# Two weight panels behind each norm multiplied with h times the scales, before the norm's factor is known

## The reference, cut to what matters

```
u = rmsnorm(h, gain) * (1 + scale) + shift      # factor = rsqrt(mean(h*h) + eps), one for each token
# feed-forward
h = h + 0.5 * (1 + gate) * ((silu(u @ wg) * (u @ wu)) @ wd)      # wg, wu: 1024 x 2816, wd: 2816 x 1024
# mixers
h = h + (1 + gate) * (mixers(u @ w_in) @ w_out)                  # w_in: 1024 x 5128
```

```
u @ w = factor * ((h * gain * (1 + scale)) @ w) + shift @ w
```

## Time and profile before

| | |
|---|---|
| median of 3 runs | 2034.93 us (2032.88 to 2040.63) |
| the profiled execution | 2039.97 us, of which the span of the profile is 2038.7 |
| mean granted clock of PE | 0.97 of full speed |
| busy: PE, DVE, ACT, POOL | 94%, 64%, 46%, 2% |
| instructions of PE | 15008 |
| DMA | 389.70 MB in 270996 packets, 57% of the engines' time in the main queue |

### The profile page before, as it was taken

The page is one execution under the profiler, slowest core; times in us unless marked ns, Lnnn a source line. Parts: engine busy times, 40 slices in busy tenths (PEclk is TensorE's granted clock), DMA queues, the critical chain, the costliest instruction groups (busy, mean ns, idle before and its releaser), DMA issues.

```text
span 2038.7 us, 33982 instructions
## 1 busy us (share of the span) xinstructions
PE 1909.3 (94%) x15008; PEld 1829.1 (90%) x15008; DVE 1311.0 (64%) x1850; ACT 942.6 (46%) x1266; POOL 43.7 (2%) x48
## 2 busy tenths in 40 slices
PE   7998988899898986999999899999999999899998
PEld 7987888898798885999899789999999999789998
DVE  4666677665776675666676856666666675755444
ACT  5564454446545443433445334334433446334333
POOL 0000100000000000000000000000000000000000
PEclk9998999999999998999989999999999999999999
DMA  9554456575363664677566345776677566334551
GB/s 291 171 190 149 160 192 223 162 256 176 129 218 127 213 216 158 210 248 249 183 214 220 134 136 186 248 248 227 211 250 248 181 212 202 104 124 145 187 186 63
DMA packets 270996, 389.70 MB, mean 191 GB/s; under 512 B 8448, under 2 KB 244224, under 8 KB 260480
## 3 DMA queue, kind: packets, MB, share of 16 engines
q1 hardware_dynamic: 270848, 387.52, 57.0%
HBM read 386.45 MB, written 1.05 MB: 190 GB/s over the span
## 4 chain that ended last, share of the span: by engine, by line
PE 69%; DVE 18%; ACT 10%; issue 1%; DMA 1%; POOL 1%; SPq 0%; DVEq 0%; ACTq 0%
PE bank L695 22%; PE bank L696 21%; PE bank L697 21%; DVE weights_split L844 6%; ACT weights_split L838 4%; PE bank L759 2%; ACT map L1279 1%; DVE xbc L2144 1%; DVE map_stat L1467 1%; ACT map L1285 1%; DVE weights L824 1%; PE bank L894 1%; DVE map L1461 1%; DVE work L792 0%; DVE a_qk_then_merged L1419 0%
## 5 line engine op out<-in xcount | busy, mean ns | idle before, releaser
L844 DVE TENSOR_TENSOR weights_split<-weights,weights_split 128x2048 fp32r<-128x2048 f32 (+2 forms) x306 | 655.2, 2141 | 434.1 <-ACT weights_split L838 433.6
L695 PE MATMUL bank<-u,weights_split 128*128 128x256 f32 x2048 | 589.7, 288 | 18.4 <-DVE u L2162 10.1
L838 ACT CAST weights_split<-weights 128x2048 fp32r<-128x2048 f32 (+2 forms) x306 | 543.1, 1776 | 136.4 <-PE bank L697 105.6
L696 PE MATMUL bank<-u,weights_split 128*128 128x256 f32 x2048 | 580.6, 283 | 0.0
L697 PE MATMUL bank<-u,weights_split 128*128 128x256 f32 x2048 | 579.5, 283 | 0.0
L695 PEld LDWEIGHTS bank<-u,weights_split 128*128 128x128 f32 x2048 | 392.0, 191 | 24.8 <-DVE u L2162 12.3
L696 PEld LDWEIGHTS bank<-u,weights_split 128*128 128x128 f32 x2048 | 394.0, 192 | 0.5 <-issue 0.5
L697 PEld LDWEIGHTS bank<-u,weights_split 128*128 128x128 f32 x2048 | 392.4, 192 | 0.0
L695 PE MATMUL bank<-y,weights_split 128*128 128x256 f32 (+1 forms) x1168 | 334.1, 286 | 4.2 <-ACT b_k L864 4.2
L696 PE MATMUL bank<-y,weights_split 128*128 128x256 f32 (+1 forms) x1168 | 330.8, 283 | 0.0
L697 PE MATMUL bank<-y,weights_split 128*128 128x256 f32 (+1 forms) x1168 | 330.0, 283 | 0.0
(11 more groups left out here) (285 smaller groups left out, 1898.5 us busy)
## 6 DMA issues: line engine op xcount, KB each, us to landing
weights<-in_ada SPq DMA_DIRECT2D x80, 1024.0 KB, 4.9
weights<-in_w_in SPq DMA_DIRECT2D x76, 1024.0 KB, 7.9
weights<-in_ffn_wg SPq DMA_DIRECT2D x44, 1024.0 KB, 5.4
weights<-in_ffn_wu SPq DMA_DIRECT2D x44, 1024.0 KB, 7.5
weights<-in_ffn_wd SPq DMA_DIRECT2D x44, 1024.0 KB, 7.2
weights<-in_w_merge SPq DMA_DIRECT2D x24, 1024.0 KB, 7.5
weights<-in_w_out SPq DMA_DIRECT2D x20, 1024.0 KB, 5.2
weights<-in_w_ple_gate SPq DMA_DIRECT2D x8, 1024.0 KB, 6.9
```

Source lines behind the costliest of these rows:

```text
L695: pe.matmul(out, left[0], right[0], start=start, stop=False, **more)
L696: pe.matmul(out, left[0], right[1], start=False, stop=False, **more)
L838: act.do.copy(split[:, 0, 0:n], raw[:, 0:n]).then_inc(*self.act_wrote.inc(("weights", key)))
L844: dve.do.tensor_tensor(split[:, 1, 0:n], raw[:, 0:n], split[:, 0, 0:n].bitcast(F32), ALU.subtract).then_inc(*self.dve_wrote.inc(("weights" ...
```

## The change

Two things are changed.

**The loads.** All weights of the plan are written into one array beforehand, panel after panel, as they stand in the buffer: a partition's part of a panel is one run of memory (8 KB for a full panel) where it was eight runs of 1 KB, or of 512 B for the panels of 128 columns.

**The norms of the six sub-layers** (not the last norm). The list has a new sequence, `boundary`:

- pending modulations are finished first (`pause_mods`)
- `raw`: for each chunk DVE adds to h, ACT rounds h times the scale into u (L2050) and squares h (L2056), DVE writes the low part (L2302). POOL adds the eight squares up (L2426). Two further columns of u hold the shifts, so a product gets the shift's share in column 256 (`u` has rows of 258 now)
- `deferred`: PE multiplies two panels at once, chunk by chunk, with this raw u, into four banks, 12 matmuls a chunk. Behind the fourth chunk it sums the squares over channels (one chunk now), behind the sixth it spreads the factor
- `modulated`: as before, but in place, u over the raw u chunk by chunk; the factor is copied out of its bank first (ACT, L2064)
- `deferred_out`: DVE copies the shift's share (L2340) and multiplies the banks by the factor (L2341); then silu and product (L2091, L2351) or copies and four convolutions with silu (L2080, L2274, L2277, L2034)
- only then `use` of the second panel, which puts the preparation of the fourth into the list

The panels are wg, wu number 0 of the feed-forwards and both of m_x for the mixers. The constants of the second model are loaded later and are waited for only by the mixers. Lines of the changed kernel: matmuls L717 to L719, a panel's cast L866 and low part L872, diagonal L820, modulations L852, adding to h L2285, u's chunks L2314, L2070, L2321.

The core of the diff:

```diff
+DEFERRED = {"ffn1": (("wg1", 0), ("wu1", 0)), "mix": (("m_x", 0), ("m_x", 1)), "ffn2": (("wg2", 0), ("wu2", 0))}
+
+SUMS_BEHIND, FACTORS_BEHIND = 3, 5
...
+    def boundary(self, before, name, l, at):
+        first, second = DEFERRED[name]
+        self.pause_mods()
         self.mods_until(72 * l + at + 2 * DC)
         self.add("coefficients", name, l, at)
-        self.run(self.norm(name, l))
+        self.add("raw", before, name, l, at)
+        self.use((*first[:1], l, *first[1:]))
+        for i in range(DC):
+            self.add("deferred", name, l, i)
+            if i == SUMS_BEHIND:
+                self.add("norm", (name, l), 0)
+            if i == FACTORS_BEHIND:
+                self.add("norm", (name, l), 1)
         self.add("modulated", name, l, at)
+        self.add("deferred_out", name, l)
+        self.use((*second[:1], l, *second[1:]))
+        self.mods_pause = False
...
-            kc = rows // P
-            sp.do.dma_start(slot[:, 0:kc * cols].rearrange("p (k n) -> p k n", k=kc),
-                            source.rearrange("(k p) n -> p k n", p=P)).then_inc(*loaded.inc((what, at)))
+            sp.do.dma_start(slot[:, 0:rows // P * cols], source).then_inc(*loaded.inc((what, at)))
...
+        if name in DEFERRED:
+            ring = self.products if name == "ffn2" else self.turned
+            return b["square_sum"], 1, 1, D, 1e-6, ring, [(self.pool_wrote, ("square_sum", tag))]
...
+        b["u_shift"] = sb("u", [P, DC, 2, T + 2], F32R)
+        b["u"] = b["u_shift"][:, :, :, 0:T]
+        b["square_sum"] = sb("square_sum", [P, 1, T])
+        b["factors"] = sb("factors", [P, T])
+        b["shift_product"] = sb("shift_product", [P, 4])
...
+    def deferred_rings(self, name):
+        if name == "ffn2":
+            return [self.scores, self.scores, self.turned, self.values]
+        return [self.products, self.products, self.spare_bank, self.values]
...
+            tag = {("wg1", 1): ("ffn1", l), ("wg2", 1): ("ffn2", l), ("m_bc", 0): ("mix", l)}.get((name, u))
+            if tag:
+                self.tensor_rows(key, b, t["u"], x_marks=[("u", tag, c) for c in range(DC)],
+                                 order=self.chunk_order(tag[0]))
...
+        pe.wait_ge(self.dve_wrote, ("raw", name, l, c))
+        for j, ring in enumerate(rings):
+            key, at = keys[j // 2], slice(j % 2 * P, (j % 2 + 1) * P)
+            hi, lo, _, _ = self.panel(key)
+            if i == 0:
+                pe.wait_ge(self.dve_wrote, ("weights", key))
+                pe.wait_ge(*ring.free(("deferred", name, l, j)))
+            last = self.parts(ring.tile(("deferred", name, l, j))[:, 0:T + 2], (hi[:, c, at], lo[:, c, at]),
+                              (u[:, c, 0, :], u[:, c, 1, :]), i == 0, i == DC - 1)
+        done = [("deferred", name, l), *(("read", key) for key in keys)] if i == DC - 1 else []
...
+    def scalar_raw(self, before, name, l, at):
+        for i, c in enumerate(self.chunk_order(name)):
+            if before:
+                act.wait_ge(self.dve_wrote, ("h2", before, c))
+            if read := self.u_read(name, l, c):
+                act.wait_ge(self.filled, read)
+            act.wait_ge(self.dve_wrote, ("coefficients", name, l))
+            act.do.activation(u[:, c, 0, 0:T], self.h[:, c, :], ACT.Copy, scale=b["coef"][:, 0, c:c + 1]).then_inc(
+                *self.act_wrote.inc(("hi", ("raw", name, l, c))))
+            if i == 0:
+                if read := self.u_read(name, l, self.chunk_order(name)[-1]):
+                    act.wait_ge(self.filled, read)
+                self.scalar_hi(u[:, :, 0, T:T + 2], self.shifts(l, at), ("raw_shift", name, l))
+            act.do.activation(b["squares"][:, c, :], self.h[:, c, :], ACT.Square).then_inc(
+                *self.act_wrote.inc(("squares", (name, l), c)))
 
...
+        ring, bank = self.factors_ring((name, l)), ("factors", (name, l), 0)
+        act.wait_ge(self.filled, bank)
+        act.do.copy(b["factors"][:, :], ring.tile(bank)[:, 0:T]).then_inc(*self.act_wrote.inc(("factors", name, l)))
...
+    def scalar_deferred_out(self, name, l):
+        if name == "mix":
+            for c in range(4):
+                act.wait_ge(self.dve_wrote, ("pad", l))
+                act.wait_ge(self.dve_wrote, ("deferred_scaled", name, l, c))
...
+                self.scaled.emptied(("deferred", l, c), self.act_wrote, ("xbc_in", l, c))
+            for c in range(4):
+                self.scalar_conv(l, c)
...
+    def vector_raw(self, before, name, l, at):
+        for i in range(DC + 1):
+            if i < DC and before:
+                self.vector_add_to_h(before, order[i])
+            if i == 1:
+                self.vector_lo(u[:, :, 1, T:T + 2], self.shifts(l, at), u[:, :, 0, T:T + 2], ("raw_shift", name, l))
+            if i > 0:
+                c = order[i - 1]
+                dve.wait_ge(self.act_wrote, ("hi", ("raw", name, l, c)))
+                dve.do.scalar_tensor_tensor(u[:, c, 1, 0:T], self.h[:, c, :], self.b["coef"][:, 0, c:c + 1],
+                                            u[:, c, 0, 0:T].bitcast(F32), ALU.mult, ALU.subtract).then_inc(
+                    *self.dve_wrote.inc(("raw", name, l, c)))
...
+    def vector_deferred_out(self, name, l):
...
+        dve.wait_ge(self.filled, ("deferred", name, l))
+        for j, ring in enumerate(rings):
+            bank = ring.tile(("deferred", name, l, j))
+            dve.do.tensor_copy(sw[:, j:j + 1], bank[:, T:T + 1]).then_inc(*self.dve_wrote.inc())
+            dve.do.tensor_tensor(to[j], bank[:, 0:T], b["factors"][:, :], ALU.mult).then_inc(
+                *self.dve_wrote.inc(("deferred_scaled", name, l, j)))
+        if name == "mix":
+            for c in range(4):
+                dve.wait_ge(self.act_wrote, ("xbc_in", l, c))
...
+        last = ("conv", l, 0) if name == "mix" else ("up", tag, 0)
+        for j, ring in enumerate(rings):
+            ring.emptied(("deferred", name, l, j), self.dve_wrote, last)
...
+                for i, c in enumerate(order[1:]):
+                    pool.wait_ge(self.act_wrote, ("squares", (name, l), c))
+                    pool.wait_ge(self.pool_wrote, LAST)
+                    pool.do.tensor_tensor(total, total if i else b["squares"][:, order[0], :], b["squares"][:, c, :],
+                                          ALU.add).then_inc(
+                        *self.pool_wrote.inc(*[("square_sum", (name, l))] * (i == DC - 2)))
```

339 lines of the change are left out of this document (210 added, 129 removed).

## The result

| | median | range | ratio to before |
|---|---|---|---|
| before | 2036.47 us | 2032.88 to 2040.63 | |
| changed | 2054.75 us | 2052.68 to 2062.80 | 1.0101, 95% interval 1.0072 to 1.0130 |

The change makes the kernel 1.0% slower; forecast were 2055 us and "slower". The ratio and its interval come from the single runs, so the ratio differs a little from that of the medians (1.0090). The profiled execution has a span of 2053.0 us, 14.3 more than before.

A forecast was written before the change was run, and what follows sets the result against it. PE's matmuls were taken as the bound (69% of the chain). Later norms + 28.6, first norm -6, loads -3, columns + 0.5 gave + 20 us: 2060 profiled, 2055 us as median; range 2042 to 2068.

The forecast's parts named there:

- Raw panels (step 1): At each norm PE starts raw matmuls 0.7 to 0.8 us after the last accumulate, then never waits between chunks.
- Third panel (2, 3): In ffn1 and mix PE stands from 16.1 to 23.7 or 24.7 us, until results free a bank.
- Fourth panel (4): Prepared only after the raw results: PE waits 4.5 us more in mix; ffn2 loses 11.8 us in all.
- Modulation rows (5): At mix of layer 0 and ffn1 of layer 1, both halves delay DVE's first add, + 2.4 us each.
- Clock (6): PE's idle stretches at each boundary cost the clock again, about 2 us; 1 in mix.
- First norm (7): At block two's first norm, raw panels need no constants, so PE works during that wait: -6 us.
- Packed loads (8): Longer weight runs save PE's waiting at the program's start only: -3 us, bounds 0 and 27.2.
- 258 columns: 576 matmuls have 258 columns instead of 256, at 0.001 us each: + 0.5 us.
- Rival A: At six boundaries the chain is shorter and the clock held, 3 to 4 us less each: 2034, no change; chance 0.17.
- B: PE's waits ahead of the third and fourth panels are half the forecast's: 2022 us, faster; chance 0.12.
- D: Packed loads save all of ACT's waits for weights as well, 25 us: 2030 us; chance 0.06.
- C: At the norms GpSimd's adds of the squares end too late, slower than forecast; size not given; chance 0.20.

## Why the prediction was right

- **Raw panels (step 1).** Forecast: start at 0.7 to 0.8 us, 2.4 more with modulation rows. Measured 1.06, 0.60 and 2.99 after T. A chunk takes DVE 0.88 us while GpSimd runs, under PE's 1.42. The forecast's 0.116 us a matmul is a little low, since a window's count takes in the matmuls across its edges; the starts give 0.1178, which is 0.3 us over the 144 matmuls of step 4.
- **Third panel (2, 3).** 16.1 to 23.7 or 24.7 us, so waits of 7.6 and 8.6. Measured 6.96 and 8.0; in mix of layer 1 the panel starts at 23.9 (24.7 forecast). The run with the own bank shows that the bank is the reason: with it PE follows u without a wait.
- **Fourth panel (4).** Forecast 34.8 us in mix and 28.5 in ffn2; measured 34.0 in mix of layer 1 and 28.1. Its wait is shorter than the 4.5 forecast: 2.41 and 2.65 us in mix, where the third panel starts at half clock and takes 7.5 to 7.7 us instead of 5.6, and 3.68 in ffn2. That it takes over when the third is helped, the run with early banks showed.
- **Modulation rows (5).** 2.4 us each: 36.4 against 34.0 us at the fourth panel of the two mixes, and 3.3 - 0.9 = 2.4 by the run that moved them, mix of layer 0 against layer 1.
- **Clock (6).** The 2 us for each boundary were an estimate of mine: in the kernel before the clock is at 0.50 from 1010 to 1013 and at 0.91 in the slice behind the earlier trace rows, and no run shows what that costs there by itself. After the change the half clock from the third panel's start is in the windows. By the starts, the 48 matmuls of the fourth panel take 1.6 to 1.7 us more than at 0.1187 in both mixes (1 forecast) and 1.6 and 2.8 in the two ffn2 (2 forecast), and those of the third in ffn1 of layer 1 take 2.0 more (2 forecast).
- **First norm (7).** -6 forecast, -7.2 measured (24.9 to 17.7). PE now waits 5.41 us there for the first raw chunk.
- **Sum of the norms.** + 28.6 forecast, 82.7 - 56.0 = + 26.7 measured.
- **Packed loads (8).** -3 forecast, -2.4 by the ratio, with zero inside the interval. That all of it lies at the start, as the forecast had it, is not shown: the two waits there went from 2.28 and 1.19 to 1.74 and 1.22.
- **258 columns.** 0.5 us forecast; here a term is missing. Their own time is 1.0 us by the run with the right addresses (0.1195 a matmul against 0.1178, 576 times). What they cost beyond it are the addresses that they give to the rows, 6 to 7 us over all products with u and y. I had asked how long two more columns take, and not where everything behind them moves to.

In the profiled pair the parts are -6.1 (end of the first model), -7.2, + 26.7, and + 0.9 for everything between the norms; sum + 14.3, where + 20 was forecast. By the medians it is + 18.3. The + 0.9 hides the addresses: behind their first four panels the four feed-forwards take 1.0 us more each, the mixers 2.6 and 0.6 less, and no run took apart what the mixers gained. So the mechanism at the norms is right, and that the time is met to the microsecond is luck: 7 us of addresses were missing, and the norms and the first model came out 6 us better than forecast.

- **Rival A** (no change) had the chains 3 to 4 us shorter per norm: they were 0.4 to 0.8 us shorter. **B** wanted PE's waits at half: those at the third panel are nearly whole, and what the fourth's in mix fall short of 4.5 went into the slower third panel. **D** has fallen with the packed loads alone.
- **C**, slower still, had GpSimd's adds end too late: they ended before DVE looked for the sum in mix; in ffn2 PE waited 0.73 us for them, and it costs nothing, since the low part ended later. With the low part behind the chain it is on the path: there PE waits 0.72 us for the adds and DVE 1.44 us for PE's sum. POOL's timeline at mix of layer 0, six adds after the first:

```profile
994.06 5.15 POOL L2426 TENSOR_TENSOR square_sum<-square_sum,squares 128x256 f32<-128x256 f32 x6
```

0.86 us each, with 0.9 taken in the forecast. (In the earlier trace rows the add did not end with the low part, but 0.47 us behind it.) DVE's pairs beside them go at 0.88 us where they take 0.79 without them (u's chunks); the instruction that reads h and u (L2302) takes 0.57 us there and 0.48 ahead of them, the one that reads a bank (L2285) 0.47 and 0.48. So the price here is 0.1 us a chunk, under 1 us a norm.

## What to carry to other kernels

Work that fills a wait of the bounding engine is worth only as much as the other engines have time for at that place: here PE's 11 idle us were filled with matmuls, and DVE, whose queue was already what PE waited for, got eight low parts, a panel's low part and the results of two panels on top, so a norm cost 13 to 21 us instead of 10 to 12. Follow the queue of the helper up to the next two pieces that the bounding engine needs (a bank, the next panel's preparation) and put those ahead of the new work; with that, a bank chosen so that the next panel has one, and the same idea gains 0.6%, or 0.8% with the addresses put right. When one of two waits in a row is taken away, expect the time in the other, and when a block of small work is moved, expect the wait at its new place.

## What the hardware showed beside it

Matmuls of 256 float32 columns in dense stretches of the second model start every 0.1178 us in the kernel before. By how far the runs moved what is multiplied against that kernel:

| | rows of u apart, bytes | y moved by, bytes | interval on u | interval on y | matmuls in 1260 to 1400 |
|---|---|---|---|---|---|
| before | 1024 | 0 | 0.1178 | 0.1178 | 1191 |
| before, tiles moved | 1032 | 144 | 0.1187 | 0.1182 | 1184 |
| changed | 1032 | 2192 | 0.1187 | 0.1182 | 1183 |
| changed, multiples of 64 | 1088 | 3136 | 0.1187 | 0.1200 | 1178 |
| before, multiples of 128 | 1152 | 2304 | 0.1178 | 0.1178 | 1191 |
| changed, multiples of 128 | 1152 | 2048 | 0.1178 | 0.1178 | 1191 |

The longer intervals are 0.3 to 1.9% longer, in no row as a wait: only the number of matmuls in a full window shows it. Moves by multiples of 128 left the intervals as they were, the others did not; no run tried more of them, none moved the weights' tiles, and why it is so is open.

During m_dt's 48 matmuls of 8 columns in layer 0 the granted clock falls to 0.50 although PE is never idle: in the changed kernel they start at full clock at 1033.4 and are at half from 1037.0 on, in the kernel before 1034.6 and 1037.1. Where a wait of 3.71 us stands ahead, they are at half from the first one, and with what follows PE stays there for 15.4 us.
